# Even-layer seams of a two-layer mixer kernel: stores, map homes, modulation and first fold placed anew

## The reference, cut to what matters

```python
h = rms_norm(x, norm_g) * (1 + sc) + sh              # modulation from silu(c) @ mod_w
u, gs, xr, gr = split(h @ w_in, 4)                   # 1024 columns each
ys = prefix_bidir(s5_scan, u)                        # 64 groups of 16 channels, 64 complex states
yr = prefix_bidir(rglru_scan, conv(xr))              # 4 heads of 256 channels
y = gelu(ys + s5_d * u)
y = y * sigmoid(y @ glu_w + glu_b)
out = concat([y * silu(gs), yr * silu(gr)]) @ w_out
x = x + gt * out
```

## Time and profile before

| | us |
|---|---|
| median of 3 runs | 2761.38 (2759.66 to 2762.35) |
| the profiled execution, its own time | 2756.0 |
| its span | 2754.4 |
| PE busy | 2570.5 (93% of the span) |
| DVE / POOL / ACT busy | 1534.2 / 982.6 / 829.9 |
| mean granted TensorE clock | 0.974 of full speed |

### The profile page before, as it was taken

How to read it: one execution, slowest core, us unless ns; L and a number is a source line. 1 busy time by engine, 2 the same in 40 slices (tenths; PEclk the granted TensorE clock), 3 DMA queues, 4 the chain that set the end, 5 groups by cost and what they waited for, 6 DMA issues and landing times.

```text
span 2754.4 us, 37624 instructions
## 1 busy us (share of the span) xinstructions
PE 2570.5 (93%) x13319; PEld 1990.4 (72%) x13319; DVE 1534.2 (56%) x2362; ACT 829.9 (30%) x997; POOL 982.6 (36%) x1163
## 2 busy tenths in 40 slices
PE   7897789999989998989999999999999989999998
PEld 3777754445445667878877877778888889887787
DVE  4677755887875224433237655866455554646510
ACT  2425634362552113222122111213233242322210
POOL 0139967887800000011233333444334433331000
PEclk9999999999999999999999999999999999999999
DMA  8312220101105776351132333474121220315421
GB/s 298 109 65 99 98 74 24 58 23 50 50 28 191 250 223 215 82 193 35 43 84 83 124 126 116 167 248 146 43 104 62 104 81 31 125 42 168 131 92 46
DMA packets 257472, 298.09 MB, mean 108 GB/s; under 512 B 34960, under 2 KB 217528, under 8 KB 256960
## 3 DMA queue, kind: packets, MB, share of 16 engines
q1 hardware_dynamic: 201568, 206.60, 23.6%
q10 hardware_dynamic: 51168, 73.04, 7.4%
q0 software_dynamic: 4608, 16.78, 1.8%
HBM read 203.09 MB, written 93.29 MB: 108 GB/s over the span
## 4 chain that ended last, share of the span: by engine, by line
PE 70%; DVE 8%; ACT 4%; issue 2%; DMA 2%; POOL 1%; ACTq 0%; DVEq 0%; SPq 0%; POOLq 0%
PE ps L135 61%; PE ps L1315 6%; DVE xc_part L2440 1%; PE ps L973 1%; ACT arena L1510 0%; ACT L1510 0%; PE ps L1320 0%; DVE arena L520 0%; PE ps L1268 0%; POOL decays L2839 0%; PE ps L1146 0%; DVE arena L2204 0%; DMA y_chunks<-arena 0%; DVE s_scan_tmp L2152 0%; DVE arena L2154 0%
## 5 line engine op out<-in xcount | busy, mean ns | idle before, releaser
L135 PE MATMUL ps<-h_full,weights 128*128 128x512 f32 (+1 forms) x1152 | 424.1, 529 | 21.0 <-DMA weights<-in_e_w_in 8.1
L135 PE MATMUL ps<-h_part,in_weight_parts 128*128 128x512 f32 (+1 forms) x1920 | 413.8, 376 | 14.2 <-DVE arena L2357 6.7
L135 PEld LDWEIGHTS ps<-h_part,in_weight_parts 128*128 128x128 f32 x1920 | 337.8, 190 | 85.7 <-issue 13.6
L135 PEld LDWEIGHTS ps<-h_full,weights 128*128 128x128 f32 x1152 | 220.8, 193 | 217.4 <-issue 204.5
L135 PE MATMUL ps<-v_part,p_part 128*128 128x512 f32 x1248 | 296.7, 397 | 0.1
L135 PEld LDWEIGHTS ps<-v_part,p_part 128*128 128x128 f32 x1248 | 235.4, 191 | 49.8 <-issue 0.9
L135 PE MATMUL ps<-q_part,xc_part 128*128 128x256 f32 x1920 | 246.9, 287 | 14.7 <-DVE v_part L2440 10.8
L135 PEld LDWEIGHTS ps<-q_part,xc_part 128*128 128x128 f32 x1920 | 236.5, 194 | 16.4 <-DVE v_part L2440 11.5
L135 PE MATMUL ps<-arena,weights 64*16 64x128 f32 (+2 forms) x896 | 180.7, 395 | 16.5 <-ACT arena L1510 14.4
L1315 PE MATMUL ps<-wo_part,mx_part 128*128 128x512 f32 x768 | 183.8, 400 | 6.9 <-DVE mx_part L2440 6.3
L1315 PEld LDWEIGHTS ps<-wo_part,mx_part 128*128 128x128 f32 x768 | 145.6, 191 | 41.3 <-issue 6.5
(11 more groups left out here) (398 smaller groups left out, 4198.0 us busy)
## 6 DMA issues: line engine op xcount, KB each, us to landing
weights<-in_e_w_in SPq DMA_DIRECT2D x32, 512.0 KB, 4.2
weights<-in_o_w_in SPq DMA_DIRECT2D x32, 512.0 KB, 4.5
s_out_maps<-arena ACTq DMA_DIRECT2D x16, 640.0 KB, 2.9
arena<-s_out_maps SPq DMA_DIRECT2D x16, 640.0 KB, 4.9
ml_xcv<-arena ACTq DMA_DIRECT2D x16, 640.0 KB, 3.0
xc_full<-ml_xcv SPq DMA_DIRECT2D x4, 2560.0 KB, 9.2
xm_tiles<-ml_xm SPq DMA_DIRECT2D x16, 640.0 KB, 3.9
weights<-in_mod_w POOLq DMA_DIRECT2D x17, 512.0 KB, 5.3
```

The costliest lines, as they stand in the source:

```text
L135: return nc.tensor.matmul(o, lhsT, rhs, start=(k == 0), stop=(k == n - 1))
```

## The change: what it does

- **State batches and branch heads.** `Ub`, `BBs` and the half of `Xw` move into W; `Vs`, `Dg` and `dcol` move into GW. SP loads `rg_w0` once the last `v_mm1` and the last even `e_mm` are done, and `rg_w1` after the last odd `e_mm`; `v_stored` is waited for only ahead of the gate weights. PE's first branch tile starts without waiting for the evacuation of the state inputs; that wait stands now ahead of its third segment.
- **Branch output.** Its store moves from ACT to SP, between the two weight loads of the next head's second kind (`branch_out(i - 1)`); the last one stands behind the first two gate weights and ahead of the first map rows.
- **First gate tile.** Segment 2 (256 columns) is computed first, ahead of the wait for ACT's last evacuation of the heads; ACT evacuates the tile into GW (`gst0`) and waits for `rg_bo` only after that.
- **Modulation.** POOL loads its weights once the branch outputs are stored; the homes are the place of `HH` and one place as before. Units per batch go from two each to 0, 2, 2, 2, 2, 2, 3, 3, 3, 3, 3, 3, 3, 1, 0, 0. `modulation_columns` follows the last batch but one.
- **Third home.** Batch 14 loads into a third home (the place of the evacuated gate tiles), and batch 15 into the even home.
- **y comes back elsewhere.** `y_full` lies where h was, so that its loads need the gate tiles done and not the states copied; five loads instead of four (the last two chunks alone). The parts lie where the states and the scan's neighbour were. ACT takes the gelu of the last two batches first, then stores both, with the first parts of y between.
- **GLU to mixer.** The mixer's operand parts 0 to 5 and its first weight are made ahead of the last GLU tile's closing; PE starts the first mixer tile after `glu_sz0` alone.
- **First fold.** `fold_transposes(0)` moves into the second mixer tile, after its sixth chunk.

```diff
@@ tiles
-        modw1 = [GW[:, 0:1024], GW[:, 1024:2048], at(42112, 1024)]
+        modw1 = [at(o, 1024) for o in (44928, 45952, 42112)]
+        MODN = [0, 2, 2, 2, 2, 2, 3, 3] + [3] * 5 + [1, 0, 0]
-        YTs = parts("y", (HTo, XTo))
+        YTs = parts("y", (XTo, YTo))
@@ SP
-            sp.wait_ge(*past("v_stored", 16 * NB))
-            sp.wait_ge(*past("e_mm0", NB // 2))
-            sp.wait_ge(*past("e_mm1", NB // 2))
+            def branch_out(i):
+                sp.wait_ge(*past("rg_bo", 2 * i + 2))
+                sp.dma_start(bo_d[2 * i:2 * i + 2].rearrange("s p t -> p s t"), HH).then_inc(sem("bo_stored"), 16)
+
+            sp.wait_ge(*past("v_mm1", NB // 2))
+            for i in range(RH):
+                for s in range(2):
+                    sp.wait_ge(*(past(f"rg_pmm{s}", 2 * i) if i else past(f"e_mm{s}", NB // 2)))
...
+                    if i and s == 0:
+                        branch_out(i - 1)
...
-            sp.wait_ge(*past("rg_bo", 2 * RH))
+            branch_out(RH - 1)
...
+            glu_weight(0)
+            sp.wait_ge(*past("gs_stored0", 64))
+            batch_rows(NB - 2, 2, "f_in2")
+            sp.wait_ge(*past("f_mm0", NB // 2 - 1))
+            batch_rows(NB - 1, 0, "f_in3")
+            sp.wait_ge(*past("gs_mm1", 12))
+            for q, (k0, n) in enumerate(((0, 2), (2, 2), (4, 2), (6, 1), (7, 1))):
+                for s in range(2):
+                    sp.wait_ge(*past(f"y_stored{s}", 16 * GB * (k0 + n)))
+                sp.dma_start(YF32[:, k0:k0 + n], y_d[k0:k0 + n].rearrange("k p t -> p k t")).then_inc(sem(f"y_in{q}"), 16)
+                if q == 0:
+                    glu_weight(1)
@@ PE
+                            if isinstance(i, int) and kind == 0 and s == 0 and t0 == 1024:
+                                pe.wait_ge(*past("wz_a", NB))
+                                pe.wait_ge(*past("wz_v", NB))
+                                pe.wait_ge(*past("v_ev", NB))
...
-            gate_rows(0, 0, (0, 2, 1))
+            gate_rows(0, 0, (2,))
+            pe.wait_ge(*past("rg_ev0", 6 * RH))
+            pe.wait_ge(*past("rg_ev1", 6 * RH))
+            gate_rows(0, 0, (0, 1))
...
-            for s in range(2):
-                pe.wait_ge(*past(f"glu_sz{s}", 4))
+            pe.wait_ge(*past("glu_sz0", 4))
             mix(0, 0, 0)
-            fold_transposes(0)
-            mix(0, 0, 1)
+            pe.wait_ge(*past("glu_sz1", 4))
+            mix(0, 0, 1, fold=0)
@@ ACT
+            outputs_taken(NB // 4 - 1, 1, 0)
+            for k in range(2):
+                outputs_high(k)
+            outputs_taken(NB // 4 - 1, 1, 1)
+            for s in range(2):
+                outputs_stored(NB // 4 - 1, 1, s)
+            outputs_high(2)
...
+            glu_weight_high(0, 1)
+            for k in range(3, DT):
+                outputs_high(k)
...
+            glu_gates(DT // 2 - 1, 0)
+            mix_weight_high(0, 0)
+            for k in range(DT - 2):
+                mixed_high(k)
+            glu_gates(DT // 2 - 1, 1)
@@ DVE
+            glu_mixed(DT // 2 - 1, 0)
+            weight_low("eo", 0, 0)
+            for k in range(DT - 2):
+                mixed_low(k)
+            glu_mixed(DT // 2 - 1, 1)
+            mixed_low(DT - 2)
+            weight_low("eo", 1, 1)
+            mixed_low(DT - 1)
@@ POOL
-            modulation_in(0)
-            modulation_in(1)
             pool.wait_ge(*past("rg_bo", 2 * RH))
-            modulation_in(2)
...
+            pool.wait_ge(*past("bo_stored", 16 * RH))
+            for n in range(3):
+                modulation_in(n)
```

More of the change, by code:

```diff
@@ L950, in outputs @@
                 b = 4 * i + 2 * z + s
-                for n in (2 * b, 2 * b + 1):
+                for n in range(sum(MODN[:b]), sum(MODN[:b + 1])):
                     modulation_unit(n)
-                pe.wait_ge(*past(f"f_in{s}", 192 * i + (96 * z + 96)))
+                x = b % 2 if b < NB - 2 else (2, 0)[s]
+                pe.wait_ge(*(past(f"f_in{s}", 192 * i + (96 * z + 96)) if b < NB - 2 else past(f"f_in{2 + s}", 96)))
                 pe.wait_ge(*past(f"z_ready{s}", 2 * i + (z + 1)))
@@ L997, in _ @@
                     outputs(NB // 4 - 1, z, s)
-            modulation_columns()
+                    if z and not s:
+                        modulation_columns()
             def three_parts(o, wp, xs, k, n):
@@ L1043, in mix @@
                     last = three_parts(ps3[s], WPs[s], xs, k, DT)
+                    if k == 5 and fold is not None:
+                        fold_transposes(fold)
                     if leaving and k < DT - 1:
@@ L1526, in gate_rows @@
                     act.wait_ge(*past(f"gs_stored{z}", 16 * i))
+                first = isinstance(i, int) and i == 0 and z == 0
+                o = gst0 if first else gst[:, z]
                 for j in js:
                     t0, n = SEGS[j]
-                    act.wait_ge(*past(f"gs_mm{z}", 3 * i + ((0, 2, 1).index(j) + 1)))
-                    nc.scalar.activation(gst[:, z, t0:t0 + n], ps[:, 4 + j, 0:n], ACT.Copy).then_inc(sem(f"gs_ev{j}"), 1)
+                    act.wait_ge(*past(f"gs_mm{z}", 3 * i + ((2, 0, 1) if first else (0, 2, 1)).index(j) + 1))
+                    nc.scalar.activation(o[:, t0:t0 + n], ps[:, 4 + j, 0:n], ACT.Copy).then_inc(sem(f"gs_ev{j}"), 1)
                 if 1 in js:
@@ L1560, in _, with high, glu_weight_high, outputs_high @@
                     outputs(2, z, s)
-            for z in range(2):
-                for s in range(2):
-                    if z == 0:
-                        gate_rows(NB // 4 - 1, 1, ((0, 2), (1,))[s])
-                    if z and s:
-                        modulation_taken(1)
-                    outputs(NB // 4 - 1, z, s)
+            def high(o, x, name):
+                nc.scalar.activation(o, x, ACT.Copy).then_inc(sem(name), 1)
+            def glu_weight_high(i, s):
+                act.wait_ge(*past(f"glu_w{s}", 16 * i + 16))
+                high(WPs[s][:, 0], Wv[:, s], "glu_wh")
+            def outputs_high(k):
+                act.wait_ge(*past(f"y_in{k // 2 if k < DT - 1 else 4}", 16))
+                high(YTs[0][:, k], YF32[:, k], "y_high")
+            for s in range(2):
+                gate_rows(NB // 4 - 1, 1, ((0, 2), (1,))[s])
+                if s:
+                    modulation_taken(1)
+                outputs(NB // 4 - 1, 0, s)
+            act.wait_ge(*past("gs_stored0", 16))
+            glu_weight_high(0, 0)
+            for s in range(2):
+                act.wait_ge(*past(f"z_ready{s}", NB // 2))
+            outputs_taken(NB // 4 - 1, 1, 0)
+            for k in range(2):
+                outputs_high(k)
+            outputs_taken(NB // 4 - 1, 1, 1)
+            for s in range(2):
+                outputs_stored(NB // 4 - 1, 1, s)
+            outputs_high(2)
+            for z in range(3):
+                act.wait_ge(*past(f"mod1_mm{z}", (11, 11, 10)[z]))
+            glu_weight_high(0, 1)
+            for k in range(3, DT):
+                outputs_high(k)
             act.wait_ge(*past("bo_stored", 16 * RH))
@@ L2712, in _ @@
             GP.memset(BI[:, :], 0.0).then_inc(sem("bi_zero"), 1)
-            for m in range(2):
-                pool.wait_ge(*past(f"rg_gmm{m}", 4 * RH))
             def modulation_in(n):
```

137 lines of the change are left out of this document (60 added, 77 removed).

## The result

Both kernels were timed side by side, five executions each:

| | before | changed |
|---|---|---|
| median, us | 2759.66 (2758.59 to 2762.35) | 2745.78 (2745.29 to 2746.97) |
| ratio | | 0.9948 [0.9934, 0.9963] |
| profiled execution, us | 2756.0 | 2745.78 |
| its span, granted clock | 2754.4 | 2744.2, 0.974 |

A forecast was written before the change was run, and what follows sets the result against it. PE, busy 93% of the span, was taken as the bound, with idle at four seams. 8.0 + 3.2 - 3.0 - 1.0 + 9.3 + 5.5 = 22.0 us off 2761.4 gave 2739.4 us, range 2727 to 2755 (the forecast's own 2733 to 2746).

The forecast's parts named there:

- rival 2: Output batches and GLU: y stores and loads collide, map rows land late; gain only 13.0 us, 2748.4; chance 0.21.
- Seam A: State batches to branch heads: first branch weight no longer waits for the lag store; gain 8.0 us, between 6 and 8.6.
- rival 4: Heads paced by DVE and ACT, mixer by its loads, so Seam A and Seam D gains are lost; 2753 to 2762; chance 0.08.
- Seam B: Heads to output batches: first gate tile evacuated earlier, batch 0 then waits for map rows; gain 3.2 us, -0.8 to 6.2.
- Modulation: Output batches 0 to 13: six more units cost 3.0 us, waits for their weights 1.0 (0 to 6).
- Seam C: Output batches to GLU: from batch 13's end, GLU tile 0 ends after 30 us instead of 39.3; gain 9.3, 4.3 to 10.9.
- I expect it landed at T + 9: T is the end of output batch 13; its y store, which batch 15's gelu waits for, lands 9 us later.
- Seam D: GLU to mixer: first mixer tile starts at once, third stalls about 3.5 us for its weight; gain 5.5, 3.5 to 10.1.
- The second half: Rest of the span from the fold ahead of the fourth mixer tile on: forecast gain 0.
- 3: Rival, output batches 6 to 12: late modulation weights become the bound; 12 us slower at 5 us per batch, 2773; chance 0.05.
- rival 1: All seams close further: earlier map rows, no modulation wait, unhindered y stores, timely mixer weight; gain 32.8 us, 2728.6; chance 0.14.

The follow-up runs named there:

- e4: Changed kernel with the mixer's third weight loaded ahead of x and its fourth ahead of the branch output: median 2737.47 us, ratio 0.9921.
- e10: Changed kernel with two modulation units ahead of every batch again, their row and columns taken around batch 15: median 2747.46 us, ratio 0.9956.
- e2: Changed kernel with four of DVE's scan steps per head moved from ahead of its second convolution to behind the L2229 products: median 2740.11 us, ratio 0.993.
- changed kernel again: The changed kernel, unedited, run and profiled a second time beside the kernel before: median 2744.66 us, ratio 0.995.
- e1: Changed kernel with the first branch weight again behind the lag store and PE again waiting for all state evacuations: median 2751.35 us, ratio 0.9973.
- e5: Changed kernel with the last branch store issued between batch 0's and batch 1's rows, not ahead of both: median 2739.55 us, ratio 0.9929.
- e3: Changed kernel with a home of its own for batch 15's gelu output, and its own store semaphore: median 2738.21 us, ratio 0.9931.
- e8: Changed kernel with the second and later loads of y issued only after batch 13's store has landed: median 2740.06 us, ratio 0.9933.
- e12: The kernel before, unchanged, profiled a second time (its "again" trace): median 2756.51 us against 2759.44 on that chip, ratio 0.9991.

## Why the prediction was right, and 8 us too large

The time, 2745.8, lies 0.2 inside the range that the prediction gave its own mechanism (2733 to 2746), with a gain that is 0.63 of the forecast one; that it lies inside is luck, since the kernel before was 1.7 faster beside it than in the runs that the forecast starts from: 2761.4 - 13.9 would be 2747.5. The sum of rival 2, 13.0, is closer to the 13.9 than 22.0 is, but by different terms: its seams B and C came out better than it says, and the heads and the second half, which it left alone, took the rest.

**Seam A** was right in its mechanism: the load took 4.04 behind `v_mm1` (4.39 assumed), PE started 1.0 and 1.5 after its last `e_mm` (1.5 forecast) and the clock stayed at 1.00. The two traces give 9.2, above the 8.6 that the prediction had as its upper end: the first four projection tiles took 68.98 where the old traces had 70.93 and 71.12, so the clock gave back 2.0 and not 1.3. Eleven traces keep this part of the change; their first marks lie from 455.9 to 460.1, a gain of 8.3 in the mean. (The prediction's 6.7 us for the weight should be 6.5, by its own figures.)

**The step that failed** is the sentence behind it, "Everything later in the heads hangs on PE and moves along", with the one in rival 4 that PE's waits in the heads are for ACT. The prediction priced the heads at nothing; they cost 3.2 in the mean. The old trace already had a wait of PE for DVE, at the third head's gates:

```profile
672.27 17.45 PE L135 MATMUL ps<-arena,weights 128*128 128x512 f32 x48 [2.10 <-DVE arena L2179]
```

Cut at this place, the heads show two losses (us; PE's waits for DVE all lie in the first stretch; e4 and e10 have the changed kernel's heads):

| | before / again | changed / again | e10 | e4 | e2 |
|---|---|---|---|---|---|
| first mark to the third head's gates | 206.6 / 206.6 | 209.3 / 207.1 | 207.1 | 207.1 | 204.2 |
| PE's waits for DVE in it | 2.1 / 2.1 | 4.6 / 2.5 | 4.1 | 0.9 | 0 |
| on to the last gate unit | 140.3 / 140.3 | 142.0 / 141.9 | 140.3 | 142.0 | 141.8 |
| the fourth head's projection in it | 69.0 / 69.0 | 70.7 / 70.7 | 69.0 | 70.7 | 70.7 |

The first stretch goes by DVE, before and after. With the changed kernel's order it takes 207.1 whether PE waits 0.9, 2.5 or 4.1 for DVE in it, since a PE that has run at a slow clock comes later and waits less; with e2's order it takes 204.2. Here the change costs 0.5; the 2.6 of the first trace did not come again. What is seen beside the 0.5, though not shown to be its cause, is that DVE's scan steps between the gates run slower. Over the same 97 us from the first mark on, the last of a step's four operations (L2154, now L2204) took 317 ns in the mean of 35 in before again, and 325 in the changed kernel again. All four operations sum to 39.2 and 39.0 us in the traces of before, and to 40.0 and 40.2 in those of the changed kernel. e1, which has the wait with the old start of PE, shows that PE's earlier start is not the cause. Why a step is slower isn't settled: POOL runs the other half of the same scan beside it, and each small operation takes either about 0.22 or 0.35 us, but no run varied that alone.

The second loss, 1.7, is a slow clock that is no longer hidden. The last gate unit of the third head and the fourth head's projection behind it, before and then in the changed kernel again:

```profile
702.20 11.89 PE L135 MATMUL ps<-arena,weights 128*128 128x512 f32 x24 [2.81 <-ACT arena L1510]
713.92 68.96 PE L135 MATMUL ps<-h_full,weights 128*128 128x512 f32 x192
```

```profile
692.91 8.86 PE L136 MATMUL ps<-arena,weights 128*128 128x512 f32 x24 [2.81 <-ACT arena L1539]
704.58 70.71 PE L136 MATMUL ps<-h_full,weights 128*128 128x512 f32 x192 [2.81 <-ACT arena L1539]
```

Before, the granted clock was 0.74 over the gate unit, which took 3.0 longer than a fast one and so only filled the 2.81 for which PE waits for ACT otherwise. In the changed kernel the unit ran fast, PE waited, and the clock fell behind the wait, to 0.77 over the first 7.4 us of the projection: 70.71 instead of 68.96, with nothing to hide it. Every trace with the changed kernel's heads has this but e10's, and e10's heads are the ones that cost only 0.5 more than the old ones. What puts the slow clock at the one place or the other stays open.

**Seam B** (1.2 for 3.2) was a wrong size. The place and the kind of the wait were forecast (8 to 10, measured 9.7). The rows land 10.9 after `rg_bo` instead of 9.7, and batch 0 behind the idle takes 6.35 (5.88 again) instead of 5.3 to 5.5. I called the load light and priced the queue by issues alone; e5 shows that the branch store ahead of the rows costs 4.3 of the wait, 2.4 of it in the pieces' landing.

**Modulation**: the six units cost 2.6 (3.0 forecast), the bunches of three no wait at all (1.0 forecast). e10 adds what the forecast left at nothing: the change's distribution is worth 2.2 and 2.6 against the even one by the traces, because the two ends, where the weights are late, carry few units.

**Seam C** (7.5 for 9.3): the step that was mis-sized is "I expect it landed at T + 9". The gelu stood at T + 13.6. The idle was therefore at the first part of y (6.56 and 0.70), not at the third (4.7), and tile 0 ended at T + 33.3 instead of T + 30. That is 6.0 less than the T + 39.3 of the first old trace; the 7.5 is a mean that the second one, slower here by 2.1, raises. The trace had shown a y store of 9.15 beside the same loads, and I discounted it because the loads start earlier; but they only last longer. This was rival 2's mechanism at part of its price. e3 and e8 show it from both sides: without the wait the gelu stands at T + 8.3, with the loads held the store is through in 4.2. The rule of the Trainium skill (DMA: Bandwidth & Descriptors, "Queues, rings and completion order") that engines take turns by packets gave T + 12 and a gain of about 7, as an estimate. The traces' T + 13.6 and 7.5 lie nearer to it than to my value; that it is the packets which decide, no run here shows, since none varied the length of a row.

**Seam D** (3.5 for 5.5): the third tile started 34.4 after the last GLU one, forecast 34.0, and the stall was 3.54, forecast 3.5. What was too small is the clock behind it: the tile took 16.3 and 15.9 where one at full clock takes 14.3, so 1.5 and 2.0 more (1.0 forecast). e4 removes the stall and with it the slow tile, 6.8 in all.

**The second half** was taken as unchanged. It took 1525.8 and 1525.7 before, 1528.2 and 1530.9 in the changed kernel, and 1525.2 to 1530.9 over the experiments, with the same instructions. One part of it is seen, 1.3 to 2.4 us of slower matmuls in the stretch shown with e12. What decides over it stays open, and with it how much of the 3.8 belongs to the change. The medians of e2, e3 and e8 moved by 2 to 4 us more than their stretches explain, within the intervals; e3's own trace, with 1530.3 in the second half, does not show where.

The rivals: 3 is excluded, modulation never waited. Rival 4's pacing by DVE is in the heads, but in the old kernel too, so that it costs 0.5 to 2.6 and not the 8.0; the mixer keeps its gain. Of rival 1 nothing came by itself, though e4 and e3 show that its gains existed: with them seam D would be 3.5 + 6.8 = 10.3 (10.1 in the rival) and seam C 7.5 + 4.5 = 12.0 (10.9).

## What to carry to other kernels

A seam is worth what its last wait leaves, and then the clock behind the idle that remains: the first work after a stall of 3 us or more was 1 to 3 us slower here, whether the stall was old or new. Before saying that an earlier start is carried through, look for any wait, however small, on an engine that runs beside the bound (DVE's 2.1 was the warning), and for stretches of slow clock that cost nothing because a wait for another engine would have stood there: they can move to where they cost. And look at what stands in the same queue just ahead of a transfer that PE will wait for, and beside it: a large store ahead of small loads cost 4.3 us and went with a few moved lines; large loads beside a small store cost 4.5, and here the cure was a home of its own for the gelu, as holding the loads back gained only 1.5.

## What the runs showed of the hardware

- A store of one batch, in rows of 640 bytes, took 10.3 from its last issue beside loads of y with rows of 5120 bytes, and 4.2 at most when most of these were held back (e8).
- Four small lag loads landed 5.3 after their last issue behind a store of 1.3 MB (2560 columns of 4 bytes on 128 partitions), and 2.9 ahead of it (e5).
- The granted clock fell to 0.55 and 0.61 in the 7 us behind idles of 9.7 and 6.6, and the mixer tile behind the idle of 3.5 took 16.3 instead of 14.3; behind idles of 1.0 and 1.5 it stayed at 1.00. Behind idles of 1.0 to 2.2 ahead of the first branch tile the first four tiles took 68.98 in ten traces, and 70.68 in one (e10, idle 1.90).
- The same slow stretch of PE in the heads cost 1.7 us in a projection and nothing in a gate unit, behind which PE waits 2.81 for ACT otherwise.
- The second half of the kernel, with the same instructions, took from 1525.2 to 1530.9 us over fourteen traces: 1525.8 and 1525.7 in two of the kernel before, 1528.2 and 1530.9 in two of the changed one.
